# Right-looking instead of left-looking inverse of the chunk triangles, in the attention stage of a transformer block

## The chip, the cores and the metric

The kernel runs on one core of one Trainium2 chip. The metric is the device time of one execution in microseconds (us); lower is better. The times that count are medians over runs; the profile is of one more execution of the same program.

The core has a matrix engine (TensorE, PE in the rows, with PEld for its weight loads), VectorE (DVE), ScalarE (ACT), GpSimd (POOL) and SyncE (SP), which here only starts transfers. Each runs its own stream of instructions in order; they meet through semaphores.

## What is computed

The reference is one transformer block on 512 tokens of width 2048: a projection of the input to 11264 columns, an attention half (stick-breaking, 16 heads of 64), a recurrent half (RWKV-7, 16 heads of 64), a mix, a norm, an expert layer and a last norm. The change touches the recurrent half, whose core is this loop over tokens:

```python
def step(state, inp):
    r_t, lw_t, k_t, v_t, a_t, b_t = inp
    sa = jnp.einsum('bhvk,bhk->bhv', state, a_t)
    state = (state * jnp.exp(lw_t)[:, :, None, :]
             + sa[..., None] * b_t[:, :, None, :]
             + v_t[..., None] * k_t[:, :, None, :])
    return state, jnp.einsum('bhvk,bhk->bhv', state, r_t)
```

The kernel does this in 8 chunks of L = 64 tokens. Inside a chunk, `sa` of a token depends on those of all earlier tokens through a strictly triangular 64 x 64 matrix A, so each pair of chunk and head needs the inverse of a unit triangular matrix. There are 8 x 16 = 128 of them, one on each of the 128 partitions.

The stage in which this inverse is worked out also computes the attention half:

```python
z = jnp.einsum('bhqd,bhkd->bhqk', q_blk, k_t).astype(jnp.float32) * scale
log_keep = jnp.where(causal, jax.nn.log_sigmoid(-z), 0.0)
log_later = lax.cumsum(log_keep, axis=3, reverse=True) - log_keep
w = jnp.where(causal, jnp.exp(jax.nn.log_sigmoid(z) + log_later), 0.0)
return jnp.einsum('bhqk,bhkd->bhqd', w.astype(v_t.dtype), v_t)
```

## The kernel before

The program is a row of stages, each a block that all engines leave before the next begins. The stage of interest is `attention_and_inverse`, from about 1000 us to 1426 us of the span. Before it stands `rwkv_prepare`, which writes the triangles to `g_d`; after it `rwkv_scan`, which reads the inverses from `wt_d`. Three pieces of work are woven together in the stage.

**The attention half.** The 16 heads go in 8 pairs p, each with two members e = 0 and 1 (`NPAIR` = 8). On PE a pair is: `sums(p, e)` (L1110, the running sums, for which it waits for POOL's masked tile `d_sp`), then, for each e, `values(p, e)` (L1120) and for the next pair `scores(p + 1, e)` (L1097 and L1102). `scores` waits for ACT's copy of the output of the pair before (`third`, L1181, tile `d_oc`). ACT turns scores into `d_na` and `d_re` (`first`, L1154 to L1166), and POOL adds these up in four instructions (L1070) and masks them (L1060) for the sums of the next pair.

**16 late blocks of the input projection** (class `Late`), 4 pieces each, so 64 pieces. A piece i is: SP loads 256 KB of weights into one of two buffers (`d_raw`, L323) once the subtraction of piece i - 2 is done; ACT makes the rounded upper half (`upper`, L337); DVE subtracts to get the lower half (`lower`, L344), which releases the buffer; PE multiplies, 12 matmuls of 128 x 512 (L102 with `d_half`). There are three pairs of halves. PE runs two pieces after each `sums` and two after each `values`/`scores` (`AFTER`), so eight per pair. ACT has the uppers of two pieces in front of each `second` and each `third`: its in-order stream puts `third` behind the upper of a piece, and this behind the load of that piece. Each block ends with a DVE copy out of PSUM (`keep`, L353) and a store.

**The inverse** (class `Inverse`) is all on DVE. The tiles `d_wt` (the inverse, set to the identity at the start) and `d_at` (A) are 64 x 64 per partition. Left-looking means: for each t from 1 to 63 column t of the inverse is made whole, from the finished columns: a product of the t x t square `wt[:, 0:t, 0:t]` with the column `at[:, 0:t, t]` into `d_prod` (L774), and a sum along its rows into `wt[:, 0:t, t]` (L777). The second operand of the product has an inner step of 64 elements, 256 bytes.

**The order on DVE** is fixed when the program is built. `pieces(0, WR)` does three lowers, then the inverse runs, and after its step t the callback `between` issues the lowers from `due[t-1]` to `due[t]`. The table `due` spreads the lowers 3 to 52 over the 63 steps in proportion to a cost per step, `t * t + 200`:

```python
cost = [0] + [t * t + 200 for t in range(1, L)]
BESIDE = PIECES * 5 // 6
due = [WR + (BESIDE - WR) * sum(cost[:t + 1]) // sum(cost) for t in range(L)]
```

The last 11 lowers follow the inverse. SP also issues, after each of the first loads, four transfers of expert weights (`move_u`, L132), and after the load of piece 56 the eight stores of the inverse (L758).

Of the kernel before, what the change touches and what calls it, by code (L numbers as in the profile page):

```python
# [6 lines left out]
P = 128  # L7
# [8 lines left out]
ALU = mybir.AluOpType  # L16
ACT = mybir.ActivationFunctionType
AX = mybir.AxisListType.X
# [17 lines left out]
class Steps:  # L36
# [3 lines left out]
    def __init__(self, eng_sem, first, names):  # L40
        self.sem, self.first, self.names = eng_sem, first, names.split()
# [325 lines left out]
L = 64  # L367
# [370 lines left out]
class Inverse:  # L738
# [4 lines left out]
    def __init__(self, sb, sem, g_d, wt_d):  # L743
        self.g_d, self.wt_d = g_d, wt_d
        self.at = sb("at", [P, L, L])
        self.wt = sb("wt", [P, L, L])
        self.prod = sb("prod", [P, L * L])
        self.a_in, self.row, self.stored = sem("a_in"), sem("row"), sem("wt_stored")

    def load(self, sp):  # L750
# [13 lines left out]
    def vector(self, dve, between):  # L764
        at, wt, row = self.at, self.wt, self.row
        dve.memset(wt[:, :, :], 0.0).then_inc(row, 1)
        dve.wait_ge(row, 1)

        dve.memset(wt[:, :, :].rearrange("p j t -> p (j t)")[:, 0:L * L:L + 1], 1.0).then_inc(row, 1)
        dve.wait_ge(row, 2)  # L770
        dve.wait_ge(self.a_in, 16 * NC)
        for t in range(1, L):
            tile = self.prod[:, 0:t * t].rearrange("p (j s) -> p j s", s=t)
            dve.tensor_tensor(tile, wt[:, 0:t, 0:t], at[:, 0:t, t].unsqueeze(1).broadcast_to([P, t, t]), ALU.mult)\  # L774
               .then_inc(row, 1)
            dve.wait_ge(row, 2 * t + 1)
            dve.tensor_reduce(wt[:, 0:t, t], tile, AX, ALU.add).then_inc(row, 1)  # L777
            between(t)
            dve.wait_ge(row, 2 * t + 2)

def rwkv_scan(nc, ar_d, bk_t_d, g_d, v_d, decay_d, wt_d, y_d):
# [168 lines left out]
def attention_and_inverse(nc, proj_t, at_d, g_d, wt_d, w_in, xt, expert_u, raw_d):  # L951
# [12 lines left out]
    with ExitStack() as ctx:  # L964
        def sb(name, shape, dt=F32):
            return ctx.enter_context(nc.sbuf_tensor("d_" + name, shape, dt))
# [34 lines left out]
            return ps[:, 3 * e + 1 + j, 3 * P:4 * P]  # L1001

        cost = [0] + [t * t + 200 for t in range(1, L)]
        BESIDE = PIECES * 5 // 6
        due = [WR + (BESIDE - WR) * sum(cost[:t + 1]) // sum(cost) for t in range(L)]

# [1626 lines left out]
def build(nc, a, out):  # L2634

    def dram(name, shape):
# [18 lines left out]
                 a["rwkv_a_lora2"], a["rwkv_g_lora1"], a["rwkv_g_lora2"],  # L2655
                 ar_d, bk_t_d, g_d, v_d, bonus_d, gate_d, cols_d, decay_d, a["w_in"], xt, a["peer_u"], raw_d)
    attention_and_inverse(nc, proj_t, at_d, g_d, wt_d, a["w_in"], xt, a["peer_u"], raw_d)
    ctx_x.close()
    rwkv_scan(nc, ar_d, bk_t_d, g_d, v_d, decay_d, wt_d, y_d)
# [51 lines left out]
```

## Time and profile before

| what | us |
|---|---|
| median of 3 runs | 4732.37 |
| lowest and highest of them | 4724.11 and 4736.43 |
| the profiled execution | 4728.67 |
| its span in the trace | 4727.0 |

Of the span PE is busy 90%, DVE 71%, ACT 33%, POOL 15%. The trace gives for each instruction its start, its length, the source line and, where its engine stood idle before it, what ended the idle time. Times of an instruction below are counted from the start of the span.
### The profile page before, as it was taken

To read this page: it belongs to the slowest core of one execution; us is meant where nothing else is said; L and a number is where in the kernel's file an instruction comes from. 1 tells how busy PE (TensorE), PEld (TensorE's weight loads), DVE (VectorE), ACT (ScalarE), POOL (GpSimd) and SP (SyncE) were. 2 spreads that over 40 slices of the span, in tenths; PEclk is the share of its full clock that TensorE was granted. 3 is DMA by queue.
4 is the path that set the end of the run, shared out by engine and by line. 5 is a ranking of instruction groups with operands and counts; after the bars stand their busy time and mean duration, and the time that the engine had idled before them with its cause. 6 is when DMAs were issued, how large, how long until landed. Compare 5 with 4: busy or idle time off the path is not lost. (4 is left out here: it accounts for less than half of the span.)

```text
span 4727.0 us, 61772 instructions
## 1 busy us (share of the span) xinstructions
PE 4270.2 (90%) x23132; PEld 3795.8 (80%) x23132; DVE 3350.5 (71%) x4949; ACT 1549.3 (33%) x2777; POOL 721.3 (15%) x613
## 2 busy tenths in 40 slices
PE   8999989979887498879987699999999999999994
PEld 6888856656667387768766699999999999999993
DVE  4444436749952543559809588888999888899997
ACT  2121204434331331132227333333333333333331
POOL 0000001114330000023450011111111111111110
PEclk9999999979899799979999899999999999999997
DMA  9999966774536447856435899999999999999995
GB/s 283 314 312 312 312 196 200 247 168 148 153 92 198 146 142 226 254 175 201 143 119 163 289 316 317 317 314 317 311 317 311 317 311 313 314 312 318 313 306 186
DMA packets 583248, 1182.07 MB, mean 250 GB/s; under 512 B 71368, under 2 KB 335408, under 8 KB 528208
## 3 DMA queue, kind: packets, MB, share of 16 engines
q1 hardware_dynamic: 513472, 811.65, 56.3%
q0 software_dynamic: 52480, 356.54, 20.7%
q10 hardware_dynamic: 17040, 10.49, 0.8%
q8 instruction: 159, 2.61, 0.2%
q14 instruction: 97, 0.79, 0.0%
HBM read 1009.07 MB, written 228.15 MB: 262 GB/s over the span
## 5 line engine op out<-in xcount | busy, mean ns | idle before, releaser
L102 PE MATMUL h_ps<-xs,h_ut 128*128 128x352 f32 x6144 | 1077.0, 324 | 36.3 <-DVE h_ut L96 36.3
L102 PE MATMUL h_ps<-h_a,h_v 128*128 128x352 f32 x6144 | 1079.8, 324 | 19.3 <-DVE h_a L96 10.1
L102 PEld LDWEIGHTS h_ps<-xs,h_ut 128*128 128x128 f32 x6144 | 1009.8, 188 | 36.8 <-DVE h_ut L96 36.8
L102 PEld LDWEIGHTS h_ps<-h_a,h_v 128*128 128x128 f32 x6144 | 1003.3, 188 | 28.7 <-DVE h_a L96 17.1
L102 PE MATMUL a_ps<-xt_hi,a_w 128*128 128x512 f32 x1792 | 553.4, 390 | 7.8 <-DVE a_w L96 7.8
L96 DVE TENSOR_TENSOR h_v<-h_v_raw,h_v 128x512 fp32r<-128x512 f32 x512 | 350.2, 684 | 73.3 <-ACT h_v L95 73.1
L102 PEld LDWEIGHTS a_ps<-xt_hi,a_w 128*128 128x128 f32 x1792 | 337.4, 188 | 78.1 <-issue 8.0
L95 ACT ACTIVATE h_v<-h_v_raw 128x512 fp32r<-128x512 f32 x512 | 318.2, 622 | 224.8 <-PE h_ps L102 224.7
L102 PE MATMUL a_ps<-xt_lo,a_w 128*128 128x512 f32 x896 | 349.3, 390 | 0.0
L2496 DVE SCALAR_TENSOR_TENSOR y_first<-h_rows,h_acts,y_first 128x2048 f32<-128x2048 f32 x128 | 300.2, 2345 | 0.0
L96 DVE TENSOR_TENSOR h_ut<-h_u_raw,h_ut 128x512 fp32r<-128x512 f32 x288 | 198.1, 688 | 134.5 <-ACT h_ut L95 134.5
L2490 DVE CUSTOM_DVE_ANT_0 h_rows<-h_rows,h_x_first 128x2048 f32<-128x2048 f32 x128 | 292.2, 2283 | 0.0
L2544 POOL DMA_INDIRECT h_rows<-in_peer_v,idx_first x128 | 123.6, 966 | 777.4 <-DVE y_few L2496 388.0
L96 DVE TENSOR_TENSOR a_w<-a_raw,a_w 128x2048 fp32r<-128x2048 f32 x56 | 127.1, 2272 | 151.9 <-ACT a_w L95 79.0
L2544 POOL DMA_INDIRECT h_rows<-in_peer_u,idx_first x128 | 123.6, 965 | 665.7 <-DVE h_acts L2490 479.3
L95 ACT ACTIVATE h_ut<-h_u_raw 128x512 fp32r<-128x512 f32 x288 | 178.4, 620 | 134.3 <-PE h_ps L102 80.9
L2481 DVE TENSOR_TENSOR yt<-yt,h_ps 128x352 f32<-128x352 f32 x403 | 201.6, 500 | 0.0
L2412 ACT ACTIVATE h_acts<-h_acts 128x1 f32<-128x1 f32 x160 | 32.0, 200 | 513.5 <-DVE h_acts L2490 513.5
L102 PEld LDWEIGHTS a_ps<-xt_lo,a_w 128*128 128x128 f32 x896 | 168.7, 188 | 35.1
L96 POOL TENSOR_TENSOR f_w<-f_raw,f_w 128x2048 fp32r<-128x2048 f32 (+1 forms) x36 | 157.4, 4376 | 216.2 <-ACT f_w L95 216.2
L95 ACT ACTIVATE h_a<-yt_last 128x352 fp32r<-128x352 f32 x128 | 63.8, 498 | 383.6 <-DVE yt_last L2465 381.1
L102 PE MATMUL d_ps<-xt_hi,d_half 128*128 128x512 f32 x512 | 178.8, 422 | 11.8 <-DVE d_half L344 11.8
(352 smaller groups left out, 6881.2 us busy)
## 6 DMA issues: line engine op xcount, KB each, us to landing
h_v_raw<-in_peer_v SPq DMA_DIRECT2D x128, 1024.0 KB, 9.0
h_u_raw<-turned_d SPq DMA_DIRECT2D x144, 512.0 KB, 9.5
a_raw<-in_w_in SPq DMA_DIRECT2D x28, 2048.0 KB, 12.3
a_xin<-in_peer_u SPq DMA_DIRECT2D x224, 256.0 KB, 7.5
turned_d<-a_xin SPq DMA_DIRECT2D x56, 1024.0 KB, 6.7
raw_d<-in_peer_u SPq DMA_DIRECT2D x448, 128.0 KB, 4.0
h_u_raw<-raw_d SPq DMA_DIRECT2D x112, 512.0 KB, 8.8
yt_last<-sums_d SPq DMA_DIRECT2D x125, 176.0 KB, 4.6
```

What stands on the lines that cost most here:

```text
L95: return act.activation(hi, whole, ACT.Copy).then_inc(done, 1)
L96: return dve.tensor_tensor(lo, whole, hi.bitcast(F32), ALU.subtract).then_inc(done, 1)
L102: mm = pe.matmul(out, lhs[a], rhs[b], start=(first and n == 0), stop=(last and n == 2))
L2412: act.activation(acts[:, j:j + 1], acts[:, j:j + 1], ACT.Gelu).then_inc(dot_gelu, 1)
L2481: dve.tensor_tensor(out, out, made, ALU.add).then_inc(y_added, 1)
L2490: dve.tensor_tensor_reduce(rows[r % RR][:, :], rows[r % RR][:, :], x1[few][:, :], 1.0, 0.0, ALU.mult, ALU.add, acts[:, j:j + 1]).then_inc( ...
L2496: dve.scalar_tensor_tensor(y[:, :], rows[r % RR][:, :], acts[:, j:j + 1], y[:, :], ALU.mult, ALU.add).then_inc(row_used, 1)
L2544: pool.indirect_dma_start(rows[r % RR][:, :], None, u_rows if of_u else v_rows, bass.IndirectOffsetOnAxis(ap=fetch_idx[few][:, c:c + 1], a ...
```

## The change

The inverse is written the other way round. After column s of the inverse is final, its product with row s of A is added at once to the rectangle of all later columns: rows 0 to s, columns s + 1 to 63. So each of the 63 steps is a multiplication into `d_prod` (now L776) and an addition in place into `d_wt` (now L779), both on (s + 1) x (63 - s) elements. The largest has 32 x 32 = 1024, and `d_prod` shrinks to a quarter. The first operand of the multiplication is now a column held still along the inner direction, and the second a contiguous piece of a row. The cost in the `due` table follows the new sizes.

```diff
-        self.prod = sb("prod", [P, L * L])
+        self.prod = sb("prod", [P, L * L // 4])
...
-        for t in range(1, L):
-            tile = self.prod[:, 0:t * t].rearrange("p (j s) -> p j s", s=t)
-            dve.tensor_tensor(tile, wt[:, 0:t, 0:t], at[:, 0:t, t].unsqueeze(1).broadcast_to([P, t, t]), ALU.mult)\
-               .then_inc(row, 1)
-            dve.wait_ge(row, 2 * t + 1)
-            dve.tensor_reduce(wt[:, 0:t, t], tile, AX, ALU.add).then_inc(row, 1)
-            between(t)
-            dve.wait_ge(row, 2 * t + 2)
+        for s in range(L - 1):
+            later = L - 1 - s
+            wide = [P, s + 1, later]
+            tile = self.prod[:, 0:(s + 1) * later].rearrange("p (j t) -> p j t", t=later)
+            dve.tensor_tensor(tile, wt[:, 0:s + 1, s].unsqueeze(2).broadcast_to(wide),
+                              at[:, s, s + 1:L].unsqueeze(1).broadcast_to(wide), ALU.mult).then_inc(row, 1)
+            dve.wait_ge(row, 2 * s + 3)
+            dve.tensor_tensor(wt[:, 0:s + 1, s + 1:L], wt[:, 0:s + 1, s + 1:L], tile, ALU.add).then_inc(row, 1)
+            between(s + 1)
+            dve.wait_ge(row, 2 * s + 4)
...
-        cost = [0] + [t * t + 200 for t in range(1, L)]
+        cost = [0] + [t * (L - t) + 200 for t in range(1, L)]
```

The streams of PE, ACT, POOL and SP are the same as before but for line numbers. Only DVE's differs. At the start of the inverse, just ahead of the first lower inside it, DVE has before (`d_prod` takes the product, `d_wt` is the inverse, `d_half` the lower half of a piece; sizes are those of the output):

```order
L774 TENSOR_TENSOR d_prod<-d_wt,d_at 128x49
L777 TENSOR_REDUCE d_wt<-d_prod 128x7
L774 TENSOR_TENSOR d_prod<-d_wt,d_at 128x64
L777 TENSOR_REDUCE d_wt<-d_prod 128x8
L774 TENSOR_TENSOR d_prod<-d_wt,d_at 128x81
L777 TENSOR_REDUCE d_wt<-d_prod 128x9
L344 TENSOR_TENSOR d_half<-d_raw,d_half 128x512
```

Now the same place on DVE reads, from the setting of the diagonal on:

```order
L769 MEMSET d_wt 128x64
L776 TENSOR_TENSOR d_prod<-d_wt,d_at 128x63
L779 TENSOR_TENSOR d_wt<-d_wt,d_prod 128x63
L776 TENSOR_TENSOR d_prod<-d_wt,d_at 128x124
L779 TENSOR_TENSOR d_wt<-d_wt,d_prod 128x2x62
L776 TENSOR_TENSOR d_prod<-d_wt,d_at 128x183
L779 TENSOR_TENSOR d_wt<-d_wt,d_prod 128x3x61
L776 TENSOR_TENSOR d_prod<-d_wt,d_at 128x240
L779 TENSOR_TENSOR d_wt<-d_wt,d_prod 128x4x60
L344 TENSOR_TENSOR d_half<-d_raw,d_half 128x512
```

The first lower moved from behind step 9 to behind step 4. The second place is on DVE around the sixth copy out of PSUM (`d_ob`), which goes with pieces 25 to 27 of the 64. Before:

```order
L344 TENSOR_TENSOR d_half<-d_raw,d_half 128x512 x2
L774 TENSOR_TENSOR d_prod<-d_wt,d_at 128x2304
L777 TENSOR_REDUCE d_wt<-d_prod 128x48
L344 TENSOR_TENSOR d_half<-d_raw,d_half 128x512
L353 COPY d_ob<-d_ps 128x512
L774 TENSOR_TENSOR d_prod<-d_wt,d_at 128x2401
L777 TENSOR_REDUCE d_wt<-d_prod 128x49
```

Now, around the same copy on DVE:

```order
L344 TENSOR_TENSOR d_half<-d_raw,d_half 128x512
L776 TENSOR_TENSOR d_prod<-d_wt,d_at 128x1023
L779 TENSOR_TENSOR d_wt<-d_wt,d_prod 128x31x33
L344 TENSOR_TENSOR d_half<-d_raw,d_half 128x512
L353 COPY d_ob<-d_ps 128x512
L776 TENSOR_TENSOR d_prod<-d_wt,d_at 128x1024
L779 TENSOR_TENSOR d_wt<-d_wt,d_prod 128x32x32
L344 TENSOR_TENSOR d_half<-d_raw,d_half 128x512
```

Here the largest steps of the new inverse stand, one between two lowers; the steps of 2304 to 3969 elements, which stand from here to the end before, are gone, and no DVE instruction of the inverse has more than 1024 elements a partition.

## Rows read from the trace of the kernel before

**Rows 1.** The page, part 1: busy time, share of the span, instructions of each engine

```profile
PE 4270.2 (90%) x23132; PEld 3795.8 (80%) x23132; DVE 3350.5 (71%) x4949; ACT 1549.3 (33%) x2777; POOL 721.3 (15%) x613
```

**Rows 2.** Busy by stretch: PE, PEld, DVE, ACT, POOL; PE clock, DMA share, GB/s

```profile
1040.16:1357.16 317.00, 275.45 (x1037) 199.97 (x1036) 305.21 (x186) 123.27 (x259) 120.98 (x72) 0.89 0.45 137
1357.16:1424.21 67.05, 65.38 (x277) 49.56 (x275) 14.67 (x20) 24.98 (x52) 11.63 (x13) 0.99 0.41 102
```

**Rows 3.** Waits, 1040 to 1357 us: waiter <- waited for: total us, times, longest

```profile
ACT d_half L337 <- DMA d_raw<-in_w_in: 96.3, 25, 7.4
...
PE d_ps L1097 <- ACT d_oc L1181: 35.1, 12, 8.8
...
DVE d_half L344 <- ACT d_half L337: 8.6, 6, 3.8
```

**Rows 4.** Groups by line, 1030 to 1430 us, DVE: busy us, mean ns of one

```profile
L774 DVE TENSOR_TENSOR d_prod<-d_wt,d_at 128x1 f32<-128x1 f32 (+62 forms) x63 | 169.9, 2696 | 0.9
...
L777 DVE TENSOR_REDUCE d_wt<-d_prod 128x1 f32<-128x1 f32 (+62 forms) x63 | 98.7, 1566 | 2.2
...
L344 DVE TENSOR_TENSOR d_half<-d_raw,d_half 128x512 fp32r<-128x512 f32 x64 | 50.3, 796 | 99.4 <-ACT d_half L337 99.4
```

**Rows 5.** Timeline of DVE, one lower in pair 1: start us, us, instruction

```profile
1100.88 0.68 DVE L344 TENSOR_TENSOR d_half<-d_raw,d_half 128x512 fp32r<-128x512 f32 x1
```

**Rows 6.** Timeline of ACT, the upper behind it, idle before in brackets

```profile
1104.88 0.63 ACT L337 ACTIVATE d_half<-d_raw 128x512 fp32r<-128x512 f32 x1 [6.41 <-DMA d_raw<-in_w_in]
```

**Rows 7.** Timeline of PE while the inverse runs, pairs 0 to 2

```profile
1040.16 1.02 PE L1110 MATMUL d_ps<-d_sp,d_tri 128*128 128x512 f32 x2
...
1106.13 0.63 PE L1097 MATMUL d_ps<-d_ident,d_qkv 128*128 128x128 f32 x2 [4.64 <-ACT d_oc L1181]
1106.68 4.63 PE L1102 MATMUL d_ps<-d_qs,d_qkv 64*128 64x512 f32 x8
...
1130.58 1.02 PE L1110 MATMUL d_ps<-d_sp,d_tri 128*128 128x512 f32 x2
```

**Rows 8.** Timeline of PE after the inverse has ended, pairs 6 and 7

```profile
1366.30 2.32 PE L1120 MATMUL d_ps<-d_w,d_vt 128*128 128x512 f32 x8
1369.43 0.41 PE L1097 MATMUL d_ps<-d_ident,d_qkv 128*128 128x128 f32 x2 [0.81 <-ACT d_oc L1181]
1369.77 2.42 PE L1102 MATMUL d_ps<-d_qs,d_qkv 64*128 64x512 f32 x8
...
1389.10 1.02 PE L1110 MATMUL d_ps<-d_sp,d_tri 128*128 128x512 f32 x2
...
1398.93 1.02 PE L1110 MATMUL d_ps<-d_sp,d_tri 128*128 128x512 f32 x2
...
1423.78 0.39 PE L102 MATMUL d_ps<-xt_hi,d_half 128*128 128x512 f32 x1
```

**Rows 9.** Groups of other stages, DVE, 1024 elements, inner operand held still

```profile
L1270 DVE TENSOR_TENSOR e_y<-e_y,e_mean x4: 1224/1224/1225, 1555.5 to 1576.3; 128x1024 f32<-128x1024 f32 x4
...
L2040 DVE TENSOR_TENSOR f_match<-f_half_f,f_iota_f x16: 1210/1222/5608, 2109.5 to 2343.8; 128x1024 f32<-128x1024 f32 x16
```

**Rows 10.** Timeline of DVE, a reduction and a product while POOL adds

```profile
1285.55 3.66 DVE L777 TENSOR_REDUCE d_wt<-d_prod 128x58 f32<-128x3364 f32 x1
...
1344.80 8.12 DVE L774 TENSOR_TENSOR d_prod<-d_wt,d_at 128x3969 f32<-128x3969 f32 x1
```

**Rows 11.** Timeline of POOL, its four additions at three places

```profile
1285.78 3.34 POOL L1070 TENSOR_TENSOR d_sp<-d_re,d_na 128x512 f32<-128x512 f32 x4 [7.70 <-ACT d_na L1166]
...
1342.71 11.22 POOL L1070 TENSOR_TENSOR d_sp<-d_re,d_na 128x512 f32<-128x512 f32 x4 [2.55 <-ACT d_na L1166]
...
1389.53 4.22 POOL L1070 TENSOR_TENSOR d_sp<-d_re,d_na 128x512 f32<-128x512 f32 x4 [6.48 <-ACT d_na L1166]
```

**Rows 12.** Timeline of PE, the sums that waited for POOL

```profile
1354.70 1.47 PE L1110 MATMUL d_ps<-d_sp,d_tri 128*128 128x512 f32 x2 [2.44 <-POOL d_sp L1060]
```

**Rows 13.** Timeline of SP, the four transfers of expert weights after a load

```profile
1102.00 2.47 SPq L132 DMA_DIRECT2D raw_d<-in_peer_u  x4
```

## The prediction

> **What bounds the kernel now.** I read the page first: PE is busy 90% of the span, DVE 71% [rows 1], so the question is whether PE waits for DVE where the change is. Busy time by stretch [rows 2] shows two regimes in this stage. From 1040.16 to 1357.16 us, while the inverse runs, DVE is busy 305.21 of 317.00 us (96%) and PE's granted clock is 0.89. From 1357.16 to 1424.21 DVE is busy 14.67 of 67.05 us and the clock is 0.99. So DVE is full until the inverse ends, and PE sets the pace after it.
>
> The waits say how a full DVE reaches PE [rows 3]. PE hardly ever waits for DVE itself; it waits 35.1 us in 12 places for ACT's copy `d_oc`, and ACT waits 96.3 us in 25 places for loads of `d_raw`. DVE waits for ACT only 8.6 us. A load may start only when the lower of two pieces earlier has freed its buffer, so ACT's wait for a load is DVE's lateness passed on. One instance: a lower on DVE starts at 1100.88 and takes 0.68, ending at 1101.56 [rows 5]; the load takes until 1104.88, when ACT, idle for 6.41 us, makes the upper [rows 6]. The copy stands behind it, and PE, idle for 4.64 us, resumes at 1106.13 [rows 7]. 
>
> The cadence gives the price. A pair has two halves with sums and two with values and scores. Undisturbed, the first kind takes 1398.93 - 1389.10 = 9.83 us, the second (1389.10 - 1366.30) / 2 = 11.40, a pair 2 x 9.83 + 2 x 11.40 = 42.46 us [rows 8]. While the inverse runs, the sums of pair 2 start at 1130.58 [rows 7] and those of pair 7 at 1389.10 [rows 8]: 258.52 / 5 = 51.7 us a pair.
>
> **The products and sums.** The change removes 63 products (169.9 us) and 63 reductions (98.7 us), 268.6 us of DVE [rows 4]. It adds 63 multiplications and 63 additions. The elements of one kind are the sum of (s + 1)(63 - s), 43,680 a partition, against 85,344 before. The price of an element is not in the trace for these very patterns, so I bound it. Near end: two products elsewhere with an operand held still along the inner direction, one of them in place, take 1.224 and 1.222 us for 1024 elements [rows 9]; with 0.68 us for 512 [rows 5] that is 1.06 ns an element and 0.14 us an instruction. Far end: the old product, whose second operand is read 256 bytes apart, took 8.12 us for 3969 elements [rows 10], 2.05 ns. I take the near end, since in both new instructions every moving operand is contiguous along the inner direction; only the last few steps have short runs. Then one kind costs 43,680 x 1.06 ns + 63 x 0.14 = 55 us, both 110. At the far end both would cost 2 x (89.5 + 8.8) = 197 us. A price below the near end has no row; it would only add idle time to DVE.
>
> **Does DVE keep up?** Beside the inverse lie 50 lowers of about 0.6 us and some 11 copies of 0.6, 37 us. DVE's load until the lower of piece 52 is 110 + 37 = 147 us (234 at the far end). PE at its own pace reaches piece 52 some 250 us after 1040. So DVE is 59% loaded (94%), and evenly, since the new costs in `due` match the new sizes. At the densest place, 1024 elements, a lower, a multiplication and an addition take 0.6 + 2 x 1.22 = 3.1 us, and PE uses a piece every 42.46 / 8 = 5.3 us. Within a group of two it uses the second 2.7 us after the first, but there are three halves, and every group is followed by 4 us or more of other matmuls, which absorb this. The stall goes to the next thing that is late, ACT's copy in its undisturbed form, with 0.8 us.
>
> **At the start** of the inverse the first lower moves from behind nine steps to behind four. Their elements are 1 to 81 before (about 4 us) and 63 to 240 now (8 x 0.14 + 2 x 610 x 1.06 ns = 2.4 us). The gain is small and is counted in pair 0's cadence below. The clearing of `d_wt` stays.
>
> **The sum.** From the sums of pair 0, e = 1, at 1040.16 [rows 7] to those of pair 7 at 1389.10 [rows 8] the kernel takes 348.94 us. At the undisturbed cadence it takes 9.83 + 22.80 + 6 x 42.46 = 287.4, which is 61.5 us less. The end, 1389.10 to 1424 [rows 8], is undisturbed already. Later stages start after this one ends and run the same instructions, so the gain passes through whole. I keep back 2 us for single lates, so 59.5 us. Against the profiled execution that is 4728.67 - 59.5 = 4669.2; that run lay 3.7 us under the median, so the forecast is 4673 us.
>
> **POOL's additions, the place where it can go wrong.** POOL makes the tile that the sums wait for. Its four additions took 3.34 us while DVE ran a reduction from 1285.55 on, but 11.22 us while DVE ran a product of 8.12 us from 1344.80 on [rows 10, 11]. The excess, 7.9 us, is about the product's length: a DVE instruction with two operands from SBUF keeps POOL out until it ends, a reduction doesn't. PE then waited 2.44 us [rows 12], and that half took 1366.30 - 1354.70 = 11.60 us instead of 9.83, so the event cost 2.44 + 1.77 = 4.2 us. The change turns every reduction into an instruction of the blocking kind, so there are 126 of them in place of 63. If DVE and POOL take turns, each of the four places between POOL's five instructions (four additions, a mask of 0.64) lets one DVE instruction in: 3.34 + 0.64 + 2 x 0.6 + 2 x 1.22 = 7.6 us. There is time for 1398.93 - 1389.53 = 9.4 us [rows 8, 11], so PE doesn't wait.
>
> The Trainium skill has a rule against this change: its page "SBUF — State Buffer", section "SBUF: two separate sides", says that VectorE and GpSimd share a pair of ports as an exclusive lock, held for the whole instruction, and that VectorE takes it for two SBUF inputs against a GpSimd operation that reads SBUF. The two places above agree. By the rule alone, with no word on turns, the price would be anything from nothing to the second rival below.
>
> **Rivals.**
> - **POOL is late in the middle** (chance 0.13). With five DVE instructions per chain and some of them waiting out a POOL addition, the chain exceeds 9.4 us in pairs 2 to 6, in one or both halves. About 6 to 8 events of 4.2 us give back 25 to 34 us: about 4702. The long chains before speak for it; that the new instructions are an eighth to a half as long speaks against it.
> - **Elements at 2.05 ns** (0.06). DVE is 94% full, and a chain is 3.98 + 1.2 + 2 x 2.2 = 9.6 us, just over its time. Some of the old lateness stays: about half of the gain, 4702.
> - **Slower: POOL is starved** (0.03). If POOL gets the ports only when DVE pauses, not between its instructions, it waits out whole bursts. From about 13 us a chain upwards all 13 remaining sums come 4 us or more late, 4 + 1.8 us each: 13 x 5.8 = 75 us against 61.5 gained, 4746 us. Against it: a chain of 11.22 us beside one long product has the length of one DVE instruction more, not two.
> - **SP is the next bound** (0.04). Behind a load it issues expert transfers for 2.47 us [rows 13], so a freed buffer can wait that long. The room between the lower and the moment its load is needed is some 6 us by the cadence, so it should hide. If not, the 0.81 us before the scores becomes 2 to 3 in each pair and takes the clock down with it: 7 x 5 = 35 us back, 4708.
> - **Nothing changes** (0.02). PE would be slow in that stretch for a reason of its own, such as the clock. The clock's rise to 0.99 just when DVE comes free speaks against it.
>
> **How the numbers follow.** The forecast, 4673 us, has 0.72. The range must take in the median's own scatter (4724 to 4736 before) below, so 4660, and most of the first two rivals above, so 4708. A difference of 0.3% (14 us) is about what a measurement can tell from no change. Faster: 0.72 + 0.13 + 0.06 + 0.04 = 0.95, less a little for what I don't see: 0.93. Same 0.03, slower 0.04.
>
> **What the changed profile should show.** Multiplications and additions of about 55 us each and 1.22 us for 1024 elements (2.2 would mean the second rival). DVE some 60% busy and waiting often for ACT's upper. The wait of PE for `d_oc` at about 0.8 us in all 14 places, 11 us in all, the clock near 0.98, sums every 42.5 us in all pairs, and the stage's last matmul near 1363 us. POOL's four additions at 5 to 8 us; PE waiting for POOL 2 us or more in several pairs would make me wrong by the first rival, an unchanged `d_oc` wait with DVE idle by the fourth.

## The result and the profile after

| | before | changed |
|---|---|---|
| median, us | 4730.94 | 4666.14 |
| lowest and highest of 4 runs | 4724.11 to 4736.43 | 4665.3 to 4671.2 |
| span of the profiled execution | 4727.0 | 4663.6 |

The ratio is 0.9866, with a 95% interval of 0.9849 to 0.9883. The forecast was 4673 us in a range of 4660 to 4708. The measured time is 7 us below the forecast and inside the range.

The page of the changed kernel, part 1 (busy time, share of the span, instructions of each engine):

```profile
span 4663.6 us, 61772 instructions
...
PE 4243.1 (91%) x23132; PEld 3780.4 (81%) x23132; DVE 3215.4 (69%) x4949; ACT 1549.7 (33%) x2777; POOL 681.9 (15%) x613
```

DVE lost 135 us of busy time, POOL 39 and PE 27, and ACT's stayed as it was. Busy time in the stretch from the sums of pair 1 to those of pair 7, changed kernel (columns as in [rows 2]):

```profile
1068.74:1326.68 257.94, 248.26 (x1033) 185.03 (x1032) 154.56 (x158) 122.71 (x259) 82.24 (x72) 0.99 0.56 161
```

DVE is busy 154.56 of 257.94 us, 60%, where it was 96%, and PE's granted clock is 0.99 where it was 0.89 [rows 2]. The waits between 1040 and 1357 us, changed kernel (waiter, waited for, us in total, times, longest), answer to [rows 3]:

```profile
DVE d_half L344 <- ACT d_half L337: 131.8, 29, 10.3
...
PE d_ps L1099 <- ACT d_oc L1183: 12.8, 14, 2.4
...
ACT d_half L337 <- DMA d_raw<-in_w_in: 9.9, 5, 2.8
```

The direction has turned round. DVE waited 8.6 us for ACT and now waits 131.8; ACT waited 96.3 us for loads and now waits 9.9; PE waited 35.1 us for the copy and now 12.8. The chain that the prediction described, lower, load, upper, copy, scores, is slack everywhere but in pair 0, where the longest wait for the copy stands (2.38 us; elsewhere it is at most 0.82).

PE's timeline shows the new cadence (start, us, instruction, idle time before it):

```profile
1031.34 1.02 PE L1112 MATMUL d_ps<-d_sp,d_tri 128*128 128x512 f32 x2
...
1045.87 0.41 PE L1099 MATMUL d_ps<-d_ident,d_qkv 128*128 128x128 f32 x2 [2.38 <-ACT d_oc L1183]
...
1068.74 1.02 PE L1112 MATMUL d_ps<-d_sp,d_tri 128*128 128x512 f32 x2
...
1111.08 1.02 PE L1112 MATMUL d_ps<-d_sp,d_tri 128*128 128x512 f32 x2
...
1326.68 1.02 PE L1112 MATMUL d_ps<-d_sp,d_tri 128*128 128x512 f32 x2
...
1361.36 0.39 PE L102 MATMUL d_ps<-xt_hi,d_half 128*128 128x512 f32 x1
```

Pair 1 takes 1111.08 - 1068.74 = 42.34 us, and all six pairs from 1 to 6 together 257.94, or 42.99 us each, against 51.7 before. The last matmul of the stage starts at 1361.36 instead of 1423.78 [rows 8], 62.4 us earlier, and the span is 63.4 us shorter. So the whole gain lies in this stage and passes through to the end, as forecast.

The groups of the new instructions (busy us, mean ns of one), changed kernel, answer to [rows 4]:

```profile
L776 DVE TENSOR_TENSOR d_prod<-d_wt,d_at 128x63 f32<-128x63 f32 (+31 forms) x63 | 69.2, 1099 | 0.6
L779 DVE TENSOR_TENSOR d_wt<-d_wt,d_prod 128x63 f32<-128x63 f32 (+31 forms) x63 | 61.1, 969 | 2.2
```

Together 130.3 us instead of 268.6.

### The profile page after: what moved, and what is told of

Its sections match the earlier page's. It is cut to its first block and busy times, and to the rows that moved or that the text cites. A ratio compares the mean times of both kernels' runs of the same rounds, so it can differ in the third digit from the quotient of the medians.

```text
span 4663.6 us, 61772 instructions
## 1 busy us (share of the span) xinstructions
PE 4243.1 (91%) x23132; PEld 3780.4 (81%) x23132; DVE 3215.4 (69%) x4949; ACT 1549.7 (33%) x2777; POOL 681.9 (15%) x613
## 5 line engine op out<-in xcount | busy, mean ns | idle before, releaser
L95 ACT ACTIVATE h_ut<-h_u_raw 128x512 fp32r<-128x512 f32 x288 | 178.4, 620 | 131.8 <-PE h_ps L102 91.2
L102 PEld LDWEIGHTS a_ps<-xt_lo,a_w 128*128 128x128 f32 x896 | 168.9, 188 | 35.1
L102 PE MATMUL b_ps<-xt_hi,b_half 128*128 128x512 f32 x512 | 177.7, 417 | 10.2 <-DVE b_half L344 10.2
```

Source lines behind the costliest of these rows:

```text
L95: return act.activation(hi, whole, ACT.Copy).then_inc(done, 1)
L102: mm = pe.matmul(out, lhs[a], rhs[b], start=(first and n == 0), stop=(last and n == 2))
```

## The experiments

All times are medians of a kernel's runs. The experiments ran on several chips, each time beside the kernel before (medians of 4724.5 to 4730.9 us). "Work" is DVE's busy time in the steps of the inverse, from the groups by line.

### Is it DVE's load, or the length of one instruction?

Two things differ at once between the kernels: the sum of DVE's work (268.6 and 130 us) and its longest instruction (8.12 and about 2 us). Three runs pull these apart. The first does every multiplication and addition twice:

```diff
+            for again in range(2):
+                dve.tensor_tensor(tile, ..., ALU.mult).then_inc(row, 1)
+                dve.wait_ge(row, 4 * s + 3 + again)
+            dve.tensor_tensor(spare, wt[:, 0:s + 1, s + 1:L], tile, ALU.add).then_inc(row, 1)
+            dve.wait_ge(row, 4 * s + 5)
             dve.tensor_tensor(wt[:, 0:s + 1, s + 1:L], wt[:, 0:s + 1, s + 1:L], tile, ALU.add).then_inc(row, 1)
```

> The right-looking inverse with each multiplication and each addition done twice (the second addition goes to a spare tile, the result is the same). DVE's work in it rises from 130 to some 260 us, as much as the 268.6 of the left-looking one, but no instruction has more than 1024 elements. Theory 'DVE's load': DVE is full again until about 1340 us, ACT waits for loads and the gain is lost, 4710 to 4735. Rival 'length of one instruction' (the old products of up to 8.1 us kept a lower or POOL waiting): the time stays within 10 us of the changed kernel, 4666 to 4676.

Measured: 4709.95 us. The groups of that run, and its waits between 1030 and 1370 us:

```profile
L779 DVE TENSOR_TENSOR d_prod<-d_wt,d_at 128x63 f32<-128x63 f32 (+31 forms) x126 | 125.0, 992 | 2.7
L784 DVE TENSOR_TENSOR d_wt<-d_wt,d_prod 128x63 f32<-128x63 f32 (+31 forms) x63 | 62.6, 994 | 2.2
L782 DVE TENSOR_TENSOR d_spare<-d_wt,d_prod 128x63 f32<-128x63 f32 (+31 forms) x63 | 60.1, 954 | 2.2
```

```profile
ACT d_half L337 <- DMA d_raw<-in_w_in: 107.7, 28, 7.1
...
PE d_ps L1104 <- ACT d_oc L1188: 24.9, 14, 4.7
```

The work is 247.7 us with no instruction over 1024 elements, and ACT again waits over 100 us for loads. 44 of the 60 us are given back. That the instructions are short doesn't save the time. (The expectation put the work at 260; it came to 248, and at the undisturbed price used below some 28 us of it stand in instructions beside POOL, where the changed kernel has 20, not in twice as much.)

The second run is the opposite, little work in long instructions: the left-looking inverse with its odd steps only.

```diff
-        for t in range(1, L):
+        for t in range(1, L):
+            if t % 2:
...
-        cost = [0] + [t * t + 200 for t in range(1, L)]
+        cost = [0] + [(t * t + 200) * (t % 2) for t in range(1, L)]
```

> The left-looking inverse with only every second step (t odd; the others are left out, so the inverse is not the reference's), the table of lowers fitted to it. DVE's work in it is 134 us, as in the changed kernel, but single steps last up to 12.4 us (product 8.1 and reduction 4.3), with 4 or 5 lowers issued in a row behind each. Theory 'DVE's load': mostly near the changed kernel, 4666 to 4690, since lowers can't be issued ahead of their buffers and so the last steps still leave gaps of 12 us in which PE uses two pieces. Rival 'length': as slow as before, 4715 to 4735.

Measured: 4683.92 us (runs from 4673 to 4689; the profiled execution was among the shortest). The work is 140 us, little more than in the changed kernel, yet some 18 us are lost. The trace is of the shortest run (4672.81 us; the other three took 4683 to 4689), so it shows only a part of them: ACT waits 54.5 us for loads in 16 places between 1030 and 1370 us, and POOL's additions next to one of the long products, in its timeline, took almost three times their own length:

```profile
1281.62 10.79 POOL L1073 TENSOR_TENSOR d_sp<-d_re,d_na 128x512 f32<-128x512 f32 x4 [16.94 <-ACT d_na L1169]
```

So something counts besides the load, though for less. It need not be the length alone: in this run a long step is followed by up to five lowers, so the lowers come in bunches too, and no run has one without the other. The third run asks whether load costs in proportion or from a knee on: only the multiplications are doubled.

> Only the multiplications of the right-looking inverse are done twice, so DVE's work in it is some 195 us, between the changed kernel (130) and the run with everything twice (248, 4710 us). Room beside the lowers is about 250 - 37 = 213 us. Theory 'there is a knee where DVE is full': still near the changed kernel, 4666 to 4678. Rival 'every us of DVE costs its share': halfway, 4685 to 4695.

Measured: 4671.96 us, with 185.6 us of work (126.8 + 58.8). DVE is 80% busy, and PE as busy as in the changed kernel (same stretch and columns as above):

```profile
1068.74:1326.68 257.94, 248.26 (x1034) 185.01 (x1033) 205.98 (x210) 122.78 (x260) 89.65 (x72) 0.99 0.56 163
```

Of 55 us more work only 4 show, beside 4667.59 us for the changed kernel on the same chip. And with no steps at all:

```diff
-            dve.tensor_tensor(tile, ..., ALU.mult).then_inc(row, 1)
-            dve.wait_ge(row, 2 * s + 3)
-            dve.tensor_tensor(wt[:, 0:s + 1, s + 1:L], ..., tile, ALU.add).then_inc(row, 1)
             between(s + 1)
```

> Leaves out the 63 steps of the inverse (the identity is stored), all lowers at their place. Theory 'DVE's load': DVE is no limit any more in the changed kernel, so this is at most 5 us faster, 4660 to 4668. Rival 'the inverse still costs something in its new form' (through POOL's additions, which are longer beside it, or through lowers that stand behind two long instructions): 10 us or more faster, under 4656.

Measured: 4669.95 us, 2 us above the expected range and no faster than the changed kernel. Its busy time in the same stretch of 257.94 us (its own pair 1 began at 1077.05, 8.3 us later than in the changed kernel's profile):

```profile
1068.74:1326.68 257.94, 248.25 (x1032) 184.97 (x1033) 53.68 (x61) 122.70 (x258) 66.05 (x74) 0.99 0.55 163
```

PE's busy time is 248.25 us against 248.26, with DVE at 53.68 instead of 154.56. Pairs 1 to 6 take 1334.97 - 1077.05 = 257.92 us without the inverse and 257.94 with it. The new inverse costs nothing there any more; it lies wholly beside PE.

In order of work the runs with an even spread read:

| run | work on DVE, us | longest instruction, elements | median, us |
|---|---|---|---|
| no inverse | 0 | - | 4669.95 |
| changed kernel (three times) | 130 | 1024 | 4666.1, 4666.2, 4667.6 |
| products twice | 186 | 1024 | 4671.96 |
| left-looking, contiguous (below) | 207 | 3969 | 4680.97 |
| everything twice | 248 | 1024 | 4709.95 |
| before | 269 | 3969 | 4724.5 to 4730.9 |

Nearly flat up to 186 us, steep above: a knee between 186 and 248, where the prediction had worked out a room of 250 - 37 = 213 us. The run at 207 us does not fix it more closely. It has instructions of up to 3969 elements, and the odd steps alone, also up to 3969, lost as much (4683.92 us) with only 140 us of work; so its 14 us over the changed kernel may come from the load or from the long steps.

### Does the table matter?

```diff
-        cost = [0] + [t * (L - t) + 200 for t in range(1, L)]
+        cost = [0] + [t * t + 200 for t in range(1, L)]
```

> The changed kernel with the old costs t * t + 200 in the table that spreads the lowers. Half of the new work is done by step 32, but the old table gives only 8 or 9 of the 50 lowers until then. Theory 'the table matters, since load must be even': lowers 5 to 18 come up to 14 us late in pairs 0 and 1, the clock drops there, 4681 to 4696. Rival 'only the total counts': 4664 to 4670.

Measured: 4697.12 us, 31 us over the changed kernel, 1 us above the expected range. With the new steps and the old table half of the gain is gone, though DVE's work is the same. PE's timeline of that run in pair 0:

```profile
1046.89 0.79 PE L102 MATMUL d_ps<-xt_hi,d_half 128*128 128x512 f32 x1 [5.91 <-DVE d_half L344]
...
1061.70 0.66 PE L1099 MATMUL d_ps<-d_ident,d_qkv 128*128 128x128 f32 x2 [7.46 <-ACT d_oc L1183]
```

Before that first wait ends DVE does nine steps, from 1037.07 to 1046.24, with no lower between them. By the starts of the sums pair 0 takes 53.9 us from e = 1 on where 32.6 would be undisturbed, and pair 1 51.3 where 42.5 would; these two make up 30 of the 31 us. From pair 2 on the cadence is undisturbed but for one fall of the clock. So the load must be even as well as under the knee.

### Fewer elements, or a better way to read them?

The product lost half of its elements and also its operand read 256 bytes apart. In this run the left-looking product reads a row of A instead of a column (so it does not compute the inverse; the work is the same in count and size):

```diff
-            dve.tensor_tensor(tile, wt[:, 0:t, 0:t], at[:, 0:t, t].unsqueeze(1).broadcast_to([P, t, t]), ALU.mult)\
+            dve.tensor_tensor(tile, wt[:, 0:t, 0:t], at[:, t, 0:t].unsqueeze(1).broadcast_to([P, t, t]), ALU.mult)\
```

> The kernel before with one index pair exchanged: the second operand of the left-looking product is read along a row of A, 4 bytes apart, instead of down a column, 256 bytes apart. It multiplies by the wrong half of A, so the inverse is not the reference's; the work is the same in count and size. If the distance in memory is what made an element cost 2 ns, the 63 products fall from 170 us to 85,344 x 1.06 ns + 9 = 99 us, DVE's work in the inverse to about 198 us, just under its room of 213 us, and the time to 4670 to 4690, a little over the run with 187 us of work (4672) for the instructions are up to 8 us long. Rival 'a product of a square costs 2 ns an element however it is read, and only the halved number of elements brought the gain': 4720 to 4732.

Measured: 4680.97 us. Its groups:

```profile
L774 DVE TENSOR_TENSOR d_prod<-d_wt,d_at 128x1 f32<-128x1 f32 (+62 forms) x63 | 108.8, 1727 | 0.9
L777 DVE TENSOR_REDUCE d_wt<-d_prod 128x1 f32<-128x1 f32 (+62 forms) x63 | 98.6, 1566 | 2.2
```

The products fall from 169.9 to 108.8 us by the way of reading alone. The product of one step, 3721 elements with POOL idle beside it, in the kernel before and in this run (timelines of DVE):

```profile
1313.88 6.54 DVE L774 TENSOR_TENSOR d_prod<-d_wt,d_at 128x3721 f32<-128x3721 f32 x1
```

```profile
1274.93 4.03 DVE L774 TENSOR_TENSOR d_prod<-d_wt,d_at 128x3721 f32<-128x3721 f32 x1
```

With the products 47 of the 60 us come back, at 207 us of work. The other half of the change alone (fewer elements, read far apart) wasn't run.

### What POOL pays

```diff
-            dve.tensor_tensor(wt[:, 0:s + 1, s + 1:L], wt[:, 0:s + 1, s + 1:L], tile, ALU.add).then_inc(row, 1)
+            dve.tensor_reduce(self.spare[:, 0:s + 1], tile, AX, ALU.add).then_inc(row, 1)
```

> Each addition is replaced by a reduction of the same product into a spare tile (so nothing is added up and the inverse stored is not the reference's). Same elements, but one operand instead of two. If an instruction with two operands from SBUF takes turns with POOL and one with a single operand doesn't, POOL's four additions in the middle of the inverse fall from 5.7 us to about 4.5, and the reduction of 1024 elements takes 1.22 us there and never 1.6. If POOL is slowed by any DVE instruction, they stay at 5.7. Time: both 4660 to 4670, since PE doesn't wait for POOL.

Measured: 4667.31 us. POOL's four additions in the middle of the inverse, first in the changed kernel, then in this run, and DVE's reduction beside the latter (timelines):

```profile
1154.00 5.76 POOL L1072 TENSOR_TENSOR d_sp<-d_re,d_na 128x512 f32<-128x512 f32 x4 [4.68 <-ACT d_na L1168]
```

```profile
1156.88 4.77 POOL L1073 TENSOR_TENSOR d_sp<-d_re,d_na 128x512 f32<-128x512 f32 x4 [5.95 <-ACT d_na L1169]
```

```profile
1160.67 1.22 DVE L780 TENSOR_REDUCE d_spare<-d_prod 128x31 f32<-128x1023 f32 x1
```

With one operand less POOL gains back 1 us of 5.76, and the reduction takes 1.22 us, its undisturbed time, while the multiplication ahead of it still took 2.01 us. The same holds in the chains of pairs 2 to 4: 5.52 to 5.76 us in the changed kernel and 4.66 to 4.77 here. So the addition's second operand costs both sides. Without any inverse (timeline of POOL, the run with no steps) the four additions take:

```profile
1152.46 4.22 POOL L1064 TENSOR_TENSOR d_sp<-d_re,d_na 128x512 f32<-128x512 f32 x4 [14.93 <-ACT d_na L1160]
```

The inverse thus costs POOL 1.5 us in the place shown, and DVE 1.2 us in the two instructions beside it (timeline of DVE beside the additions at 1154.00, and 7 us later, when POOL is idle):

```profile
1155.02 0.81 DVE L344 TENSOR_TENSOR d_half<-d_raw,d_half 128x512 fp32r<-128x512 f32 x1 [3.38 <-ACT d_half L337]
1155.76 2.01 DVE L776 TENSOR_TENSOR d_prod<-d_wt,d_at 128x1023 f32<-128x1023 f32 x1
1157.80 1.64 DVE L779 TENSOR_TENSOR d_wt<-d_wt,d_prod 128x1023 f32<-128x1023 f32 x1
...
1164.25 1.22 DVE L776 TENSOR_TENSOR d_prod<-d_wt,d_at 128x1023 f32<-128x1023 f32 x1
1165.50 1.22 DVE L779 TENSOR_TENSOR d_wt<-d_wt,d_prod 128x1023 f32<-128x1023 f32 x1
```

### The start of the stage

In the two profiles the start differed by something that the change can't touch: ACT waited 11.83 us for the queries of pair 1 before and 5.34 us after. So the changed kernel ran twice more.

> The changed kernel once more, on the chip of the next three runs, for comparison. Both theories: 4666 us (4660 to 4672). What is open is the start of the stage: in the profile of the changed kernel ACT waited 5.34 us for the queries of pair 1, in that of before 11.83 us, though the program is the same up to there. If this is scatter of the transfers, the wait will differ again here, and the time will move by up to 6 us with it; if the change causes it, it stays at 5 to 6 us.

> The changed kernel beside the two above, for comparison on the same chip: 4661 to 4671.

Measured: 4666.18 and 4667.59 us. The wait was 6.53 us in the first and, by ACT's timeline, 12.30 in the second:

```profile
1030.12 0.63 ACT L1150 ACTIVATE d_qs<-d_qkv 128x512 f32<-128x512 f32 x1 [12.30 <-DMA d_qkv<-proj_t]
```

So the change doesn't cause it; the same program scatters like this. It hardly moves the time: in the second run the sums of pair 0, e = 1, started at 1039.81, 8.5 us later than in the changed kernel's first profile, but the sums of pair 1 at 1072.37, only 3.6 us later, because pair 0 then ran undisturbed, 32.56 us. Most of an early start is lost again in pair 0.

Three attempts were made to win that start. The first issues the load of pair 1 ahead of the loads of the triangles, the second also starts the expert transfers 8 pieces later, the third issues the triangles' loads one by one behind piece loads and gives DVE 12 lowers ahead of the first step:

```diff
             for i in range(RR):
                 late.load(sp, i)
-            inverse.load(sp)
             load(1)
...
-                if i - RR < 2 * (MOVED - MOVED_BESIDE_RWKV):
-                    move_u(sp, expert_u, raw_d, 2 * MOVED_BESIDE_RWKV + i - RR, u_moved)
+                if i - RR < NC:
+                    inverse.load(sp, i - RR)
+                if NC <= i - RR < NC + 2 * (MOVED - MOVED_BESIDE_RWKV):
+                    move_u(sp, expert_u, raw_d, 2 * MOVED_BESIDE_RWKV + i - RR - NC, u_moved)
```

> The changed kernel with the load of pair 1 issued ahead of the eight loads of the triangles, two lines exchanged. Theory 'PE's first piece waits for ACT, and ACT for this load': ACT's wait for the queries (5.34 us) goes, the first piece starts 5 us earlier or more, 4655 to 4663. Rival: the triangles come later by as much and DVE's start with them, nothing won, 4664 to 4668.

> As the run before, and the transfers of expert weights start 8 pieces later. In the changed kernel the copy in pair 0 is 2.38 us late, and its upper waits for a load that stands behind four such transfers (2.47 us). Theory 'SP's queue is the limit in pair 0 only': the 2.38 becomes 0.8, and the clock stays up behind it, 4 us less than the run before, 4650 to 4660. Rival: no difference, since the load was late for its buffer.

> An attempt to better both kernels. The eight loads of the triangles, which hold SP for 16 to 22 us at the start of the stage, are issued one behind each of eight piece loads, ahead of the expert transfers; the clearing of the inverse is done first, and DVE makes 12 lowers before the first step. DVE then has the same 130 us of steps beside 41 lowers instead of 50. Theory 'pair 0 is held up by SP's queue': the first piece starts at about 1023 us and pair 0 runs at the undisturbed pace, sums of pair 1 near 1062 us instead of 1069 to 1072, 4655 to 4662. Rival 'the transfers themselves are the limit there, whatever their order': no better than the changed kernel, 4664 to 4670. Rival 'DVE is now too full': ACT waits for loads in later pairs, over 4675.

Measured: 4665.86, 4665.03 and 4667.99 us, all within the scatter of the changed kernel; three misses for the theory that SP's order holds up pair 0. In each the first part did what it should (ACT's wait for the queries is gone), and then pair 0 waited for pieces. In the second the late copy is gone too (PE waits 0.76 us for it instead of 2.38), but PE's timeline has a new wait for a lower:

```profile
1042.77 0.79 PE L102 MATMUL d_ps<-xt_hi,d_half 128*128 128x512 f32 x1 [5.17 <-DVE d_half L344]
```

DVE was 95% busy there, from 1036 to 1050 us, with the clearing of `d_wt` (3.47 us) and the first steps ahead of that lower, while the transfers kept only 22% of the DMA engines' time busy. In the third, where the clearing comes early and DVE is 19% busy in that stretch, PE's and ACT's timelines have:

```profile
1048.62 0.66 PE L1103 MATMUL d_ps<-d_ident,d_qkv 128*128 128x128 f32 x2 [6.78 <-ACT d_oc L1187]
```

```profile
1033.58 0.63 ACT L337 ACTIVATE d_half<-d_raw 128x512 fp32r<-128x512 f32 x1 [5.97 <-DMA d_raw<-in_w_in]
```

The sums of pair 1 start at 1072.54, 1071.32 and 1071.98 us, and at 1068.74 to 1072.37 in the three profiles of the changed kernel, whether pair 0's began at 1030 or at 1040. So at least two things stand close together there, DVE's clearing and first steps in the second attempt and slow loads in the third (there the piece loads between 990 and 1060 us took 6.9 us to land in the median, 3.9 in the changed kernel). What sets the time in the changed kernel was not settled. No version was found that beats the changed kernel.

## Why the prediction was right

**DVE full, passed on through the loads: right.** DVE's wait for ACT rose from 8.6 to 131.8 us and ACT's for loads fell from 96.3 to 9.9. The runs with DVE's work raised again brought the waits back.

**The sum: right in total, with two errors that cancel.** The prediction took 287.4 us from the sums of pair 0, e = 1, to those of pair 7. The first profile has 1326.68 - 1031.34 = 295.3 us, 7.9 more: 4.8 in pair 0, whose copy came 2.38 us late and took the clock down, and twice 1.6 us for a drop of the clock. But it also began 8.8 us earlier than before, which no term of the sum had. That these two cancel is luck. The third run of the changed kernel shows the sum without it (timeline of PE, the sums of pair 0, e = 1, of pair 1 and of pair 7):

```profile
1039.81 1.02 PE L1112 MATMUL d_ps<-d_sp,d_tri 128*128 128x512 f32 x2
...
1072.37 1.02 PE L1112 MATMUL d_ps<-d_sp,d_tri 128*128 128x512 f32 x2
...
1328.72 1.02 PE L1112 MATMUL d_ps<-d_sp,d_tri 128*128 128x512 f32 x2
```

It began where the kernel before did and took 288.9 us, one drop of the clock more than forecast. The reserve of 2 us was of the right size; the 7 us between forecast and median are this reserve, the 1 us won outside, and the scatter of medians (that of before moved by 6 us between groups of runs).

**Does DVE keep up: right, with the load put too low.** 147 us against 250 gave 59%. The 60% of the stretch above agree only because that stretch begins behind pair 0, where DVE is full, and runs on past the last step. From the first step (1034.64) to the lower of piece 52 (1295.69, to its end) DVE is busy 172.6 of 261.7 us, 66%. The margin was wide enough for the 26 us that the forecast left out. The room of 213 us lies where the table of runs has the knee, between 186 and 248.

**The products: a little too cheap.** 55 us each were forecast, 69.2 and 61.1 measured. The price of an element was right (1.22 us for 1023 elements when POOL is idle), though the two instructions elsewhere that it came from are a subtraction and a comparison, not products. Of the 20 us above this price 19.6 stand in steps that run beside a POOL instruction and 0.5 in all the others, so it is waiting for POOL, which the sum for DVE had left out. The far end was wrong in the other direction: 2.05 ns an element came from a product of 8.12 us that itself ran beside POOL; the one of 6.54 us has 1.76. The contiguous left-looking run puts the effect of reading 256 bytes apart at 61 us of products over 85,344 elements, so about 0.7 ns on top of 1.06.

**The start.** Behind four steps instead of nine, the first lower inside the inverse came 2.8 us after the diagonal was set, against 4.3 before. Whether it won anything is not shown.

**The rivals.** POOL was never late: its additions took at most 5.76 us where turns gave 3.34 + 3.6 = 7 without the mask and the limit was 9.4. The rule that a two-operand instruction keeps POOL out until it ends was too strict for short ones: between 1154.00 and 1159.76 POOL's additions (3.34 us where DVE leaves them alone) and DVE's lower, multiplication and addition (0.60 + 2 x 1.22) went by, 6.4 us of work in 5.76. So the two overlap somewhat. The Trainium skill's "SBUF — State Buffer", section "SBUF: two separate sides", speaks of an exclusive lock for a whole instruction; by that rule the old long products fit (11.22 us beside one of 8.12), and the short ones come out at 6.4 us or more where 5.76 were measured. SP shows as a limit only in pair 0: the 2.38 us went with the expert transfers moved later, but the time did not. The rivals "elements at 2 ns", "starved" and "nothing changes" find no support.

**What the prediction had not weighed.** The table's share. It was counted as a condition ("evenly, since the new costs fit") and not priced; with the old table 31 us of the gain are gone. Pair 0 is the other: the late copy and the fallen clock there cost 4.8 us, where the sum had its undisturbed cadence.

## What to carry to other kernels

An in-order engine that frees buffers for loads must be judged by its share of the time between two uses, not by who waits for it: here PE hardly waited for DVE, yet 96% busy on DVE cost 60 us through loads, copies and the clock, while 80% cost only 4 us and 60% nothing. Before shortening such work further, find the knee; past it there is nothing to win (no inverse at all was not faster). And when the size of the steps changes, the table that weaves other work between them must change with it: with the old table half the gain is lost.

## What was not expected of the hardware

- PE's clock fell to its lower level behind an idle time of 0.82 us, which had left it up in most other places. PE's timeline, changed kernel; the first matmul behind the scores takes 0.79 us instead of 0.50, and 1.6 us are lost:

```profile
1262.93 0.41 PE L1099 MATMUL d_ps<-d_ident,d_qkv 128*128 128x128 f32 x2 [0.82 <-ACT d_oc L1183]
1263.27 2.62 PE L1104 MATMUL d_ps<-d_qs,d_qkv 64*128 64x512 f32 x8
1265.82 0.79 PE L102 MATMUL d_ps<-xt_hi,d_half 128*128 128x512 f32 x1
```

  It came once or twice among pairs 1 to 6 of most profiles: here in pairs 3 and 5, in both further profiles of the changed kernel in pair 5 alone. Where it came twice in the changed kernel, with the products twice and with no inverse, the two lie 75.1 us apart each time. What sets it off is open.
- Two DVE instructions of 1.22 us beside POOL's additions became 2.01 and 1.64 us while POOL's 3.34 us became 5.76: each side pays for the other, but with the lower beside them the sum is less than if only one could run at a time (6.4 us of work in 5.76).
- The eight loads of the triangles took SP 15.9, 17.6 and 19.7 us to issue in the three profiles of the changed kernel, and ACT's wait for the load behind them was 5.34, 6.53 and 12.30 us. With no inverse, where SP's stream is the same but for what it waits for, they took 22.1 us.
